# A hybrid decoder step on one core: late squares, an early root table, a last down group by chunk, and attention output cut in halves

## The reference, cut to what matters

```python
xn = rmsnorm(h, g_pool)                          # front: pooling mixer
h  = h + pool_mixer(ext(xn), w_pool, pool_scale)
h  = h + (relu(rmsnorm(h, g_mlp[0]) @ w_up[0]) ** 2) @ w_down[0]
k, v, logf = shared_kv(h)                        # K, V and forget gates
q  = rmsnorm_heads(rmsnorm(h, g_attn) @ w_q)
h  = h + attend(q, k, v, logf) @ w_o             # causal, with decay
h  = h + (relu(rmsnorm(h, g_mlp[1]) @ w_up[1]) ** 2) @ w_down[1]
# outputs: h, the last pooling inputs, k, v, logf
```

## Time and profile before

| | us |
|---|---|
| median of 3 runs | 2351.63 |
| the profiled execution, its own time | 2349.69 |
| its span | 2347.9 |
| PE busy | 2284.9 (97%) |
| DVE, ACT, POOL busy | 1033.8, 581.4, 632.4 |

### The profile page before, as it was taken

One profiled execution on the slowest core, in us unless ns is written; L12 is line 12 of the kernel. 1 busy time (PEld: TensorE's weight loads), 2 busy tenths in 40 slices (PEclk: granted clock), 3 DMA queues, 4 the chain that ended last, 5 costly groups with the idle time before them and its releaser, 6 DMA issues. The chain is left out here.

```text
span 2347.9 us, 36305 instructions
## 1 busy us (share of the span) xinstructions
PE 2284.9 (97%) x14220; PEld 2093.6 (89%) x14220; DVE 1033.8 (44%) x1728; ACT 581.4 (25%) x1270; POOL 632.4 (27%) x444
## 2 busy tenths in 40 slices
PE   7999999999999999999989999999999999999998
PEld 7999999999999967777756666799999999999997
DVE  6743332433433756442146777434433323333331
ACT  6420110110100433332135666322110100101101
POOL 6622222232332512100000110453222323222221
PEclk9999999999999999999999999999999999999999
DMA  4111111111111214444464554111111111111111
GB/s 140 40 46 54 46 46 46 46 46 46 46 46 46 90 54 150 134 147 143 155 182 96 126 114 100 36 46 46 45 46 46 46 46 46 46 46 51 48 46 75
DMA packets 194328, 169.96 MB, mean 72 GB/s; under 512 B 28608, under 2 KB 168944, under 8 KB 194167
## 3 DMA queue, kind: packets, MB, share of 16 engines
q1 hardware_dynamic: 153225, 137.71, 20.4%
q10 hardware_dynamic: 40950, 30.02, 4.0%
HBM read 137.55 MB, written 30.50 MB: 72 GB/s over the span
## 5 line engine op out<-in xcount | busy, mean ns | idle before, releaser
L341 PE MATMUL ps<-xn_hi,w_lo 128*128 128x352 f32 x1536 | 497.1, 324 | 5.0 <-DVE h L564 3.2
L494 PE MATMUL ps<-hid_hi,w_lo 128*128 128x352 f32 x1536 | 495.4, 323 | 0.0
L494 PE MATMUL ps<-hid_lo,w_hi 128*128 128x352 f32 x1536 | 492.7, 321 | 0.0
L341 PE MATMUL ps<-xn_lo,w_hi 128*128 128x352 f32 x1536 | 492.4, 321 | 0.0
L341 PE MATMUL ps<-xn_hi,w_hi 128*128 128x352 f32 x1536 | 492.3, 320 | 0.0
L494 PE MATMUL ps<-hid_hi,w_hi 128*128 128x352 f32 x1536 | 492.2, 320 | 0.0
L318 POOL CAST w_hi<-w_raw 128x1024 fp32r<-128x1024 f32 x136 | 142.8, 1050 | 1008.0 <-issue 529.0
L564 DVE TENSOR_TENSOR h<-ps,h 128x352 f32<-128x352 f32 x384 | 198.5, 522 | 446.3 <-PE ps L494 446.3
L532 ACT ACTIVATE tmp_b<-tmp_a 128x352 f32<-128x352 f32 x192 | 95.1, 499 | 1090.6 <-DVE tmp_a L550 1090.6
L320 POOL TENSOR_TENSOR w_lo<-w_raw,w_hi 128x1024 fp32r<-128x1024 f32 x136 | 328.4, 2415 | 10.9
L341 PEld LDWEIGHTS ps<-xn_hi,w_lo 128*128 128x128 f32 x1536 | 288.1, 188 | 7.3 <-DVE h L564 4.3
(11 more groups left out here) (228 smaller groups left out, 2577.4 us busy)
## 6 DMA issues: line engine op xcount, KB each, us to landing
w_raw<-in_w_up SPq DMA_DIRECT2D x64, 512.0 KB, 4.0
w_raw<-in_w_down SPq DMA_DIRECT2D x64, 512.0 KB, 3.4
out<-tok_out ACTq DMA_DIRECT2D x32, 256.0 KB, 2.1
qk_dram<-turn_hi ACTq DMA_DIRECT2D x32, 256.0 KB, 2.4
qk_dram<-turn_lo ACTq DMA_DIRECT2D x32, 256.0 KB, 2.9
k_page<-in_cache_k SPq DMA_DIRECT2D x32, 256.0 KB, 3.3
v_page<-in_cache_v SPq DMA_DIRECT2D x16, 512.0 KB, 9.2
q_a<-qk_dram SPq DMA_DIRECT2D x32, 256.0 KB
```

The source lines that it names most:

```text
L341: last = pe.matmul(ps[:, bank, 0:CH], w, x(k, c), start=(k == 0 and i == 0), stop=(k == nk - 1 and i == 2))
L494: last = pe.matmul(ps[:, NC * (dm % 2) + c, 0:CH], w, x, start=(k == 0 and i == 0), stop=(k == GT - 1 and i == 2))
```

## The change

1. The first MLP's squares (`prep[0]`, `by_chunk`) are no longer made beside `xn_hi`. ACT makes those of chunk 0 between the `xn_hi` tiles of chunks 1 and 2 and the last eight behind them; 16 buffers instead of 3; the 21 sums are made by DVE behind all `xn_lo` tiles. POOL makes no sums in the front, and splits the first two blocks of MLP 0 at `i = 8` and `i = 9`.
2. ACT runs a root on a constant before its first square.
3. The last down group of MLP 1 runs chunk by chunk, `dm` inside, with all four weight blocks in buffers of their own in the place of `xn`; the transposes of each output tile follow one product behind; ACT and DVE copy them out and SP sends pieces of 512 channels by up to 128 tokens. The weights of this group are loaded once all up blocks are done.
4. The attention output is cut in halves of 512 columns, the first half at the sixth copy of a pair. Chunk 0 of the projection's first tile needs only first halves, chunk 1 all.
5. Semaphores of small outputs are merged.

```diff
-            def pool_tile(self, pool, q):
+            def act_square(self, act, q):
+                m, c = self.tile(q)
+                if m and self.sum_at(m, c) >= len(self.slots):
+                    act.wait_ge(self.acc, self.sum_at(m, c) - len(self.slots) + 1)
+                sq = self.slots[self.sum_at(m, c) % len(self.slots)] if m else tmp_b[:, c, :]
+                act.activation(sq, h[:, m, chunk(c)], ACT.Square).then_inc(self.sq, 1)
...
+            def sum_tile(self, eng, q):       # as pool_tile, on DVE for prep[0]
...
@@ front_act
+                    act.activation(x_rt[:, NX + 1:NX + 2], eps_c[:, 0:1], ACT.Sqrt, ...).then_inc(x_root, 1)
...
+            act.wait_ge(band_full, 2 * NX + 2)
+            act.wait_ge(pool_lo, NX + 1)
             for q in range(KT, NC * KT):
                 prep[0].act_tile(act, q)
+                prep[0].act_square(act, q - KT)
+            for q in range((NC - 1) * KT, NC * KT):
+                prep[0].act_square(act, q)
@@ front_pool
-                if i in (3, 4):
-                    split_one(pool, i - 3)
-                if 7 <= i:
-                    for q in range(2 * (i - 7), 2 * (i - 7) + 2):
-                        prep[0].pool_tile(pool, q)
+                if i in (3, 4, NX - 1, NX):
+                    split_one(pool, (3, 4, NX - 1, NX).index(i))
@@ front_dve
+            for q in range(NC * KT):
+                prep[0].sum_tile(dve, q)
             for c in range(NC):
                 prep[0].dve_rec(dve, c)
@@ weights_in
+                if l == 1:
+                    sp.wait_ge(mlps[1].up_full, NC * GT * NG)
@@ LastDown.pe
+                def main(n):                                  # product n of 24: c, dm = divmod(n, KT)
+                    pe.wait_ge(mlp.added, self.BASE + (n - 1 if n >= 2 else n - 5))
+                    if c == 0 and dm % 2 == 0:
+                        pe.wait_ge(w_split, 2 * (n_blocks - GT + dm // 2) + 2)
...                                                           # 12 matmuls into bank n % 2
+                def turn(n):                                  # 3 transposes: 128, 128 and 96 tokens
+                    pe.wait_ge(mlp.added, self.BASE + n + 1)
...
+                for n in range(NC * KT):
+                    main(n)
+                    if n:
+                        turn(n - 1)
+                turn(NC * KT - 1)
@@ prompt_pool
-            def cut_o_pair(r):
-                pool.wait_ge(o_ev, 8 * (r + 1))
-                cut_o(r + 1 if r else 0, r, slice(0, T))
+            def cut_o_pair(r, g):
+                pool.wait_ge(o_ev, 8 * r + 6 + 2 * g)
+                cut_o(2 * r + g + (1 if r else 0), r, slice(512 * g, 512 * g + 512))
@@ ProjO
-                            before = lambda k: pe.wait_ge(o_cut, 2 + 2 * (k + 1))
+                            before = lambda k: pe.wait_ge(o_cut, 2 * (2 * k + 1) + (2 if k else 0))
+                        elif par == 0 and c == 1:
+                            pe.wait_ge(o_cut, 4 * NP + 2)
```

More of the change, by code:

```diff
@@ L153, in decoder_step @@
         cnt_r = front("cnt_r", [P, 16])
-        x_ss, x_rt, x_rr = (front(n, [P, NX + 1]) for n in ("x_ss", "x_rt", "x_rr"))
+        x_ss, x_rt, x_rr = (front(n, [P, NX + 2]) for n in ("x_ss", "x_rt", "x_rr"))
         assert b_at <= d2_at + KT * N * 4
+        sq_x = [at(f"sq_x{i}", [P, CH], F32, d_at + 4 * D + i * CH * 4) for i in range(8)]
+        sq_p = [at(f"sq_p{i}", [P, CH], F32, pooled_at + i * CH * 4) for i in range(5)]
         square_out = at("square_out", [P, D], F32, rms_at)
@@ L325, in split_one, with split_end @@
                         pw_hi if n < 2 else w_hi, pw_lo if n < 2 else w_lo)
+        def split_end(pool):
+            pool.wait_ge(end_in, 16 * GT)
+            for q in range(GT):
+                n = n_blocks - GT + q
+                pool.tensor_copy(end_hi[:, q, :], end_raw[:, q, :]).then_inc(w_split, 1)
+                pool.wait_ge(w_split, n * 2 + 1)
+                pool.tensor_tensor(end_lo[:, q, :], end_raw[:, q, :], end_hi[:, q, :].bitcast(F32),
+                                   ALU.subtract).then_inc(w_split, 1)
         def split_weights(pool, n0, count):
@@ L360, in decoder_step, with __init__ @@
         class Prep:
-            def __init__(self, name, gain, ready, clear=None, base=0, by_chunk=False):
+            def __init__(self, name, gain, ready, clear=None, base=0, by_chunk=False, slots=None):
+                self.slots = [tmp_a[:, c, :] for c in range(NC)] + [t[:, :] for t in slots or ()]
                 self.gain, self.ready, self.clear, self.base, self.by_chunk = gain, ready, clear, base, by_chunk
@@ L476, in down @@
                     pe.wait_ge(self.lo, g * (3 * GT) + 3 * GT)
+                    if self.end and isinstance(g, int) and g == NG - 1:
+                        self.end.pe(pe, self, hidden)
+                        return
                     for dm in range(KT):
@@ L506, in pe @@
                 self.two_a_turn(pe, up, down)
-                pe.drain().then_inc(w_used, 1)
+                if not self.end:
+                    pe.drain().then_inc(w_used, 1)
             def two_a_turn(self, eng, up, down):
@@ L557, in down @@
                 def down(g, slot):
+                    if self.end and isinstance(g, int) and g == NG - 1:
+                        self.end.dve(dve, self)
+                        return
                     for dm in range(KT):
@@ L1849, in _ @@
             mlps[1].pe(pe)
-            pe.wait_ge(mlps[1].added, 3 * KT * NG)
-            for t in range(NTT):
-                w = min(P, N - t * P)
-                for b in range(2):
-                    n = 2 * t + b
-                    if n >= 4:
-                        pe.wait_ge(y_cp, n - 3)
-                    for k in range(4):
-                        last = pe.transpose(ps[0:w, n % 4, k * P:(k + 1) * P], h[:, 4 * b + k, t * P:t * P + w],
-                                            ident[:, :])
-                    last.then_inc(y_tr, 1)
         @block.scalar
@@ L1878, in _ @@
             mlps[1].act(act)
[L1879 to L1890 removed]
+            last_down.act(act)
         @block.vector
```

171 lines of the change are left out of this document (117 added, 54 removed).

## The result

The changed kernel takes 2329.23 us (median of 4 runs, 2326.25 to 2330.33), the kernel before 2351.43 beside it (4 runs): ratio 0.9902, 95% interval 0.9887 to 0.9917. 2326.3 had been predicted, in a range of 2322 to 2338. The medians lie 22.2 us apart. In the profiles the span fell from 2347.9 to 2327.3 us, by 20.6 where the three sums had 25.3. The table tells where. Each column is a stage between two rows of the trace; "low" is how long the granted clock was at its lower level, 1.2 GHz, in the front's band products (19 to 33 us), in the mix (55 to 67) and ahead of the attention (1189 to 1221), added up from stretches of half a microsecond.

The account below looks back on a forecast made before the run. PE, busy for 97% of the span, bounds the kernel, so only its waits or needless work can give. 5.0 + 9.3 + 11.0 = 25.3 us off 2349.69 gives 2324.4; from the median 2351.63, 2326.3 us, range 2322 to 2338.

Parts of the forecast that it names:

- the three sums: Predicted gains at the front (5.0 us), the tail (9.3) and the attention with the step to the projection (11.0): 25.3 us.
- Sum C: Attention and step to the output projection: halved cuts end POOL's hold on p_lo sooner, gaining 11.0 us.
- halves do not pay: Rival in the attention, chance 0.18: p_lo meeting any POOL instruction counts; gain near 5 us, time 2332 us.
- Sum B: Tail: 22.5 us behind the last product go, 7.9 of transposes between products and 5.3 behind come: 9.3 us gained.
- Sum A: Front: earlier root table, no POOL sums and DVE free sooner, less 0.3 for late sums: 5.0 us gained, bounds 1.0 to 6.0.
- The root first: Front: a root on a constant puts ACT's table load under the DMA wait, gaining 2.5 us, bounds 1.0 to 2.6.
- 0.51 us and 0.03 for its own semaphore, 0.54, so 11.4 us: Front, DVE: pitch of the 21 dependent sums of squares, taking them from 73.4 to 84.9 us.
- margin of 1 us: MLP 0's first block: DVE's first relu ready at 94.9 us, PE asking for it at 96.1, so it fits by about 1 us.
- POOL's split: MLP 0: POOL's next split starts at 84.8 us, 0.8 behind PE's second block, just as the last sum of squares ends.
- the sums' chain becomes the bound: Rival in the front, chance 0.12: DVE's sums of squares run late, the front keeps 1 to 2.5 us, time about 2329.
- The closed middle: Stretches where PE's matmuls run without a gap (MLP 0 from its third block, K/V/Q projections, MLP 1): the change touches nothing there.

Follow-up runs that it names:

- fill_wait: Changed kernel with 34 useless transposes of the identity on PE where it waits 4.3 us for v_new, ahead of the first weighing: 2327.03 us.
- turns_twice: Changed kernel with each transpose of the last down group issued twice, 72 transposes more, same results: 2336.59 us.
- sums_free: Changed kernel with POOL's split of MLP 0's third block waiting until all 21 sums of the squares are done: 2326.79 us.
- a_undone: Changed kernel with the front as before: no root on a constant first, squares beside xn_hi, sums by POOL, splits as before: 2331.84 us.
- adds_first: Changed kernel with DVE's two xn_lo tiles of the last front step queued behind the mix's next adds instead of ahead of them: 2327.26 us.

## Why the prediction was right, and where it was not

- *Sum C, 11.0: right.* 11.23 in the profile, 11.20 by undoing it. Pairs of heads take 33.01 (predicted 33.0), `p_lo` at the cut 1.15 (1.3), the projection starts with no wait. No cost of the first half shows: a pair takes what two heads without a cut took, 32.96. The rival that halves do not pay is out.
- *Sum B, 9.3: right.* 9.8 in the profile, 9.0 by undoing it. The turns cost 0.34 each, 0.113 a transpose (0.12), and 5.6 us lie behind the last product (5.3). The group stayed at clock 1.00. The Trainium skill, TensorE: Matmul & The Clock Gate, PE-mode transpose, by which transposes do not count as busy in the same way, is not borne out: in the profile of fill_wait 34 transposes in the place of the wait left the clock at 1.00, and turns_twice kept it with a quarter of the group's time in them. The second is the weaker evidence, since products fill the rest.
- *Sum A, 5.0: wrong in size.* 2.49 in the first profile, 0.25 in the second (MLP 0's first down product at 168.27 and 170.51, for 170.76), where the front ran 3.4 us longer at the lower clock; by undoing it, 3.2 and 1.0. The root first holds, and MLP 0 did start at 71.57 (71.7) where the clock was as before. The step that failed is "0.51 us and 0.03 for its own semaphore, 0.54, so 11.4 us": a sum that waits for the one before starts 0.63 behind it, 0.52 for the addition and 0.10, not 0.03, for the wait. Over the chain the mean is 0.60, 1.3 us more for 21 sums, and they began 0.7 later than I had. That used up the margin of 1 us. POOL's split, at 84.77 as predicted (84.8), fell on the last five sums (2.6 more), and the rival "the sums' chain becomes the bound" came true at about the price named for it, 2.5 us: 1.3 at the third up block and 1.3 at the third total. sums_free gave 2.8 back. Its chance, 0.12, was too small: behind a chain of 27 instructions a margin of 1 us is gone with an error of 0.04 us in each.
- *The closed middle: wrong.* "The change touches these four and nothing in the closed middle" overlooked an open place in it, PE's 4.1 us for `v_new`, and what follows: 2.7 us lost to the clock. That the loss is the clock and that it falls because PE stands still is shown: in each of the ten profiles in which PE waits 4.0 us or more there a low stretch follows, and in fill_wait, where the wait is filled, none does. That the change causes the longer low time is not shown. There is one profile of before, with 6.8 us; the changed kernel had 13.6 both times, but turns_twice, which does the same work up to the last group, had 10.2 (so 30.75 us for this stage, 1.0 more than before and not 2.7), and so had the old front in a_undone. What sets it is open.
- The total: A lost 2.5, the stretch ahead of the attention 2.7 and the rest of the middle 0.25, while B and C gave 0.7 more than said: 25.3 - 2.5 - 2.9 + 0.7 = 20.6, 4.7 short. The medians miss by only 2.9 (2329.23 for 2326.3), since the profiled execution of before was 1.7 us quicker than its median and that of the changed kernel was not. That is inside the range, which was wide enough for one sum to fail; it is no confirmation of A.

## What to carry to other kernels

Look at every long wait of TensorE (here 4.0 to 5.3 us) together with the granted clock of the stretch behind it: filling the wait with useful work that needs nothing of what is awaited pays twice (7.2 us for a wait of 4.3 here), and even useless work paid 5.3. When a chain of small dependent operations moves to VectorE, take its measured pitch with the wait inside, interleave two chains, and keep GpSimd's casts and subtractions away from it by a wait rather than by a margin. Cutting a GpSimd instruction in two was worth 11.2 us here: what counted was where its end falls.

## What the hardware showed beyond that

- An addition of 352 columns that waits for the one before it on VectorE comes 0.63 us after it; with another between, 0.435 us, less than the 0.52 that its row shows as a duration.
- A cast by GpSimd, with one SBUF operand, holds VectorE's additions too. In adds_first one addition starts beside the cast:

```profile
84.90 1.17 DVE L440 TENSOR_TENSOR tmp_b<-tmp_b,tmp_a 128x352 f32<-128x352 f32 x1
84.35 1.35 POOL L330 CAST w_hi<-w_raw 128x1024 fp32r<-128x1024 f32 x1 [23.40 <-PE ps L363]
85.78 2.54 POOL L332 TENSOR_TENSOR w_lo<-w_raw,w_hi 128x1024 fp32r<-128x1024 f32 x1
```

  Alone it takes 0.52 and would be done at 85.4, before the subtraction starts, yet it ends at 86.07, 0.37 us behind the cast. The sum behind it ends 0.38 us behind the subtraction (88.70 for 88.32). In the changed kernel it is the same: 0.37 behind the cast, 0.38 behind the subtraction. The Trainium skill, GPSIMD Engine Reference, Specifications, says that GpSimd shares its SBUF interfaces with VectorE and contends with VectorE's instructions that have two SBUF inputs, as these additions have; both cases agree with it.
- The time at the lower clock differed between two profiles of one kernel (3.4 and 6.8 us in the front), and with it went about 2 us of this kernel's time. So a part worth less is better read from its stage than from the median, and beside a profile with the same low time.
